# Four convolution shifts given to VectorE, the group norm ahead of the convolution's mean, quarter state updates and head sums in two parts

## The reference

```python
for l in range(2):
    x = x + 0.5 * swiglu(rms_norm(x), ...)           # 1024 -> 2816 -> 1024
    proj = rms_norm(x) @ w_in[l]                     # 2944 columns
    y_rwkv = rwkv7(token_shift(proj[:, :1280]))      # 6 heads of 64, recurrent state 64x64 a head
    y_attn = attention(proj[:, 1280:2432])           # 6 heads, q and k normed by head, 3 dilations
    y_conv = conv_mixer(proj[:, 2432:])              # 256 channels, causal depthwise, 31 taps
    x = x + concat(y_rwkv, y_attn, y_conv) @ w_out[l]
    x = x + 0.5 * swiglu(rms_norm(x), ...)

# rwkv step
state = state * w_t + (state @ a_t) b_t + v_t k_t ; y_t = state @ r_t
# then y is normed by head (mean and variance over 64), scaled, added to a bonus and gated
# conv_mixer
z = u[:, :256] * sigmoid(u[:, 256:])
z = sum_j w[j] * z shifted by (30 - j) tokens, plus a bias
z = silu(layer_norm(z))                              # over the 256 channels
```

## Time and profile before

| | |
|---|---|
| time, median of 3 runs | 1419.99 us (1418.55 to 1420.47) |
| profiled execution | 1419.94 us, of which the span is 1417.9 us |
| PE busy | 1375.2 us, 97% of the span |
| DVE busy | 937.0 us, 66% |
| ACT busy | 721.9 us, 51% |
| POOL busy | 172.5 us, 12%, 169 instructions |
| chain that ended last, by engine | PE 79%, POOL 10%, DVE 5%, ACT 3%, issue 2% |

### The profile page before, as it was taken

How to read it: one execution, slowest core, us unless ns; L and a number is a source line. 1 busy time by engine, 2 the same in 40 slices (tenths; PEclk the granted TensorE clock), 3 DMA queues, 4 the chain that set the end, 5 groups by cost and what they waited for, 6 DMA issues and landing times.

```text
span 1417.9 us, 25201 instructions
## 1 busy us (share of the span) xinstructions
PE 1375.2 (97%) x10047; PEld 1211.3 (85%) x10047; DVE 937.0 (66%) x1211; ACT 721.9 (51%) x992; POOL 172.5 (12%) x169
## 2 busy tenths in 40 slices
PE   8999999998999999999999999999999999999997
PEld 7888889977788888888888988788888898899996
DVE  5656666684766556665656766576565675887677
ACT  6444466454654445644447655464444445554442
POOL 3000000198000000000000059400000033000000
PEclk9999999999999999999999999999999999999999
DMA  9756365200676545755519210275562943455540
GB/s 339 249 180 201 98 202 163 82 18 2 218 253 199 185 144 180 247 191 179 176 65 297 75 61 3 87 258 193 186 198 100 315 154 116 149 186 199 179 147 30
DMA packets 172516, 230.58 MB, mean 163 GB/s; under 512 B 4671, under 2 KB 153847, under 8 KB 172181
## 3 DMA queue, kind: packets, MB, share of 16 engines
q1 hardware_dynamic: 169952, 223.75, 48.0%
q10 hardware_dynamic: 1877, 5.59, 1.0%
q0 software_dynamic: 608, 0.12, 0.0%
HBM read 228.39 MB, written 2.63 MB: 163 GB/s over the span
## 4 chain that ended last, share of the span: by engine, by line
PE 79%; POOL 10%; DVE 5%; ACT 3%; issue 2%; DMA 0%; POOLq 0%; DVEq 0%; ACTq 0%
PE bank L473 42%; PE bank L593 22%; PE bank L595 11%; POOL mix L1875 4%; POOL proj L1873 4%; ACT hT L870 1%; POOL mix L1869 1%; DVE up_lo L458 1%; ACT up_hi L453 1%; DVE down_lo L458 1%; PE bank L1161 1%; PE bank L1209 1%; DVE work L784 0%; DVE x L758 0%; PE bank L841 0%
## 5 line engine op out<-in xcount | busy, mean ns | idle before, releaser
L458 DVE TENSOR_TENSOR down_lo<-w_down,down_hi 128x2048 fp32r<-128x2048 f32 x67 | 155.3, 2318 | 100.5 <-ACT down_hi L453 100.5
L676 ACT ACTIVATE work<-bank 128x256 f32<-128x256 f32 x176 | 66.7, 384 | 266.8 <-PE bank L595 257.6
L453 ACT ACTIVATE down_hi<-w_down 128x2048 fp32r<-128x2048 f32 x67 | 128.6, 1919 | 121.4 <-PE bank L473 120.3
L458 DVE TENSOR_TENSOR gate_lo<-w_gate,gate_hi 128x2048 fp32r<-128x2048 f32 x67 | 153.9, 2297 | 53.1 <-ACT gate_hi L453 52.9
L593 PE MATMUL bank<-hT,up_hi 128*128 128x512 f32 x704 | 176.7, 393 | 0.8 <-DVE up_lo L458 0.8
L458 DVE TENSOR_TENSOR up_lo<-w_up,up_hi 128x2048 fp32r<-128x2048 f32 x72 | 162.4, 2256 | 17.0 <-ACT up_hi L453 17.0
L593 PE MATMUL bank<-hT,gate_hi 128*128 128x512 f32 x640 | 159.3, 391 | 0.0
L473 PE MATMUL bank<-down_hi,ff_hi 128*128 128x512 f32 x400 | 156.3, 391 | 0.0
L473 PE MATMUL bank<-down_lo,ff_hi 128*128 128x512 f32 x400 | 156.3, 391 | 0.0
L473 PE MATMUL bank<-down_hi,ff_lo 128*128 128x512 f32 x400 | 155.7, 389 | 0.0
L725 DVE TENSOR_TENSOR work<-bank,work 128x256 f32<-128x256 f32 x176 | 73.0, 420 | 114.5 <-ACT work L676 114.5
(11 more groups left out here) (340 smaller groups left out, 2389.0 us busy)
## 6 DMA issues: line engine op xcount, KB each, us to landing
w_gate<-in_ffn_w_gate_dram SPq DMA_DIRECT2D x44, 1024.0 KB, 5.4
w_up<-in_ffn_w_up_dram SPq DMA_DIRECT2D x44, 1024.0 KB, 5.4
w_down<-in_ffn_w_down_dram SPq DMA_DIRECT2D x44, 1024.0 KB, 5.1
w_up<-in_w_in_dram SPq DMA_DIRECT2D x12, 1024.0 KB, 9.5
w_down<-in_w_in_dram SPq DMA_DIRECT2D x11, 1024.0 KB, 6.4
w_gate<-in_w_up_dram SPq DMA_DIRECT2D x11, 1024.0 KB, 5.1
w_up<-in_w_up_dram SPq DMA_DIRECT2D x11, 1024.0 KB, 5.1
w_down<-in_w_down_dram SPq DMA_DIRECT2D x11, 1024.0 KB, 5.2
```

The lines of the kernel that those rows point to most:

```text
L453: act.activation(staged[kind][0][:, 0:cols], slot[sl][:, 0:cols], ACT.Copy).then_inc(high[sl], 1)
L458: dve.tensor_tensor(staged[kind][1][:, 0:cols], slot[sl][:, 0:cols], staged[kind][0][:, 0:cols].bitcast(F32), ALU.subtract).then_inc(split ...
L676: act.activation(low[:, q, j * SEQ:(j + 1) * SEQ], psum[2 * q + j][:, SEQ:], ACT.Copy)\
```

## The change

Line numbers in the changed file differ. The parts are:

1. Shifts 6 to 9 leave POOL. DVE computes them (`side_tap`) into `parts[1]`: the first as a product, the others as product and addition in one instruction, two channel blocks each. Two shifts follow the state update of chunk 0 and two that of chunk 1. POOL adds `parts[1]` to `acc` at its end.
2. In the output, PE does unit 1, `gn_spread(0)`, unit 2 and `gn_spread(1)` first, and the mean of the convolution after them. DVE subtracts that mean after the group norm's products. ACT squares both parities before it takes the first root. `cl_ready` is now `conv_dve`, with one more signal.
3. The state update goes by quarters. PE forms only the 64x64 block of each head (six products where there were three), DVE multiplies the two diagonal quarters with half the partitions each, `state` is cleared beforehand (a memset of 1152 columns), and `cend` shrinks from three arrays of 384 columns to one copy of 9.
4. The head sums of q stand in the middle of tile 8 and those of k in the middle of tile 9. `qk_sum` follows the latter.

```diff
--- before
+++ after
...
@@ -309,2 +309,3 @@
         SCALED_LAGS = (1, 2, 3, 4, 5)
+        SIDE_LAGS = (6, 7, 8, 9)
         parts = [proj[:, K + 1:K + 3, 1:], proj[:, V:V + 2, 1:]]
@@ -330,3 +331,3 @@
         satok, o = area(o, NT, 384)
-        cend, o = area(o_bh, 3, 3, P)
+        cend, o = area(o_bh, 3, 3)
         state, o = area(o, 3, 3, P)
@@ -1248,7 +1249,9 @@
             ones_product(pe, 4, bonus).then_inc(S["bonus_mm"], 1)
-            pe_tile(pe, uses, 8, n_norm)
+            def qk_sums(i):
+                return head_sums(pe, psum[3][:, 12 * i:12 * i + 12], lambda c, t: qsq[:, 3 * i + c, tokens(t)])
+
+            pe_tile(pe, uses, 8, n_norm, (0,))
             pe.wait_ge(S["qk_sq"], 1 + past["qk_sq"])
-            for i in range(2):
-                mm = head_sums(pe, psum[3][:, 12 * i:12 * i + 12], lambda c, t: qsq[:, 3 * i + c, tokens(t)])
-            mm.then_inc(S["qk_sum"], 1)
+            qk_sums(0)
+            pe_tile(pe, uses, 8, n_norm, (1,))
             pe.wait_ge(S["kk_ready"], 1 + past["kk_ready"])
@@ -1263,3 +1266,5 @@
                     mm.then_inc(S["a_mm"], 1)
-            pe_tile(pe, uses, 9, n_norm)
+            pe_tile(pe, uses, 9, n_norm, (0,))
+            qk_sums(1).then_inc(S["qk_sum"], 1)
+            pe_tile(pe, uses, 9, n_norm, (1,))
 
@@ -1400,11 +1405,9 @@
                                   stop=False, skip_group_check=True)
-                    for pr in range(3):
-                        at = slice(pr * P, (pr + 1) * P)
-                        pe.matmul(bank[:, at], tok[2][rows_, t, at], tok[3][rows_, t, at], start=(ch == 0 and pr == 0),
-                                  stop=False, skip_group_check=True)
+                    for h in range(NH1):
+                        pe.matmul(bank[half(h), head(h)], tok[2][rows_, t, head(h)], tok[3][rows_, t, head(h)],
+                                  start=(ch == 0 and h < 2), stop=False, skip_group_check=True)
                     pe.wait_ge(S["sa_done"], ch + 1 + past["sa_done"])
-                    for pr in range(3):
-                        at = slice(pr * P, (pr + 1) * P)
-                        mm = pe.matmul(bank[:, at], tok[1][rows_, t, at], satok[rows_, t, at], start=False, stop=True,
-                                       skip_group_check=True)
+                    for h in range(NH1):
+                        mm = pe.matmul(bank[half(h), head(h)], tok[1][rows_, t, head(h)],
+                                       satok[rows_, t, head(h)], start=False, stop=True, skip_group_check=True)
                     mm.then_inc(S["st_mm"], 1)
@@ -1457,3 +1460,6 @@
             variance(1)
+            out_unit(0, 1)
             gn_spread(0)
+            out_unit(0, 2)
+            gn_spread(1)
             pe.wait_ge(S["conv_acc"], 1 + past["conv_acc"])
@@ -1463,5 +1469,3 @@
             mm.then_inc(S["cl_mean"], 1)
-            out_unit(0, 1)
-            gn_spread(1)
-            for i in range(2, 7):
+            for i in range(3, 7):
                 out_unit(0, i)
@@ -1624,2 +1628,3 @@
                    .then_inc(S["y_sq"], 1)
+            for k in range(2):
                 act.wait_ge(S["gn_var"], k + 1 + past["gn_var"])
@@ -1637,3 +1642,3 @@
             act_high(act, uses, OUT_SLOTS[3], 0, 1)
-            act.wait_ge(S["cl_ready"], 2 + past["cl_ready"])
+            act.wait_ge(S["conv_dve"], 3 + past["conv_dve"])
             for c in range(2):
@@ -1794,9 +1799,19 @@
                     attention.normalise(h + 1)
-                if i in (19, 20, 21):
-                    c = i - 19
-                    if c == 0:
-                        dve.wait_ge(S["copy_done"], COPIES - 6 + past["copy_done"])
-                    end = ec[:, :, (c + 1) * CHUNK - 1:(c + 1) * CHUNK].broadcast_to([P, 3, P])
-                    dve.tensor_tensor(cend[:, c], end, pairs.unsqueeze(1).broadcast_to([P, 3, P]), mult)\
-                       .then_inc(S["cend_ready"], 1)
+                if i == 19:
+                    dve.wait_ge(S["copy_done"], COPIES - 6 + past["copy_done"])
+                    ends = ec.rearrange("p c (k n) -> p k c n", n=CHUNK)[:, 0:3, :, CHUNK - 1]
+                    dve.tensor_copy(cend, ends)
+                    dve.memset(state, 0.0).then_inc(S["cend_ready"], 1)
+
+            def side_tap(i):
+                lag = SIDE_LAGS[i]
+                for c in range(2):
+                    to, z, w = parts[1][:, c, lag:], proj[:, CU + c, 1:1 + SEQ - lag], col("conv_dw_w", 2 * (CONV_W - 1 - lag) + c)
+                    if i == 0:
+                        ins = dve.tensor_scalar(to, z, w, None, mult)
+                    else:
+                        ins = dve.scalar_tensor_tensor(to, z, w, to, mult, add)
+                if i + 1 < len(SIDE_LAGS):
+                    link(ins)
+                return ins
 
@@ -1807,5 +1822,16 @@
                 if ch == 0:
-                    dve.wait_ge(S["cend_ready"], 3 + past["cend_ready"])
-                dve.tensor_tensor(state[:, ch], src, cend[:, ch], mult).then_inc(S["st_done"], 1)
+                    dve.wait_ge(S["cend_ready"], 1 + past["cend_ready"])
+                for r in (half(0), half(1)):
+                    ins = dve.tensor_tensor(state[r, ch, :, r], src[r, :, r], cend[r, ch].unsqueeze(2).broadcast_to([CHUNK, 3, CHUNK]),
+                                            mult)
+                ins.then_inc(S["st_done"], 1)
                 dve.wait_ge(S["st_done"], ch + 1 + past["st_done"])
+                if ch == 0:
+                    dve.wait_ge(S["conv_added"], 2 + past["conv_added"])
+                    dve.memset(parts[1][:, :, 0:SIDE_LAGS[0]], 0.0)
+                    side_tap(0)
+                    side_tap(1)
+                if ch == 1:
+                    side_tap(2)
+                    side_tap(3).then_inc(S["conv_dve"], 1)
                 if ch == 2:
@@ -1823,6 +1849,2 @@
                                 over_heads(gnst[:, 6 * k:6 * k + 6], NH1)).then_inc(S["gn_rows"], 1)
-            dve.wait_ge(S["cl_mean"], 1 + past["cl_mean"])
-            for c in range(2):
-                ins = dve.scalar_tensor_tensor(mix[:, 6 + c, :], psum[0][:, 0:SEQ], -1.0 / 256, mix[:, 6 + c, :], mult, add)
-            ins.then_inc(S["cl_ready"], 1)
             for k in range(2):
@@ -1832,2 +1854,6 @@
                 dve.tensor_tensor(parity(mix[:, 0:3, :])[:, k], view, parity(bonus)[:, k], add).then_inc(S["mixr_ready"], 1)
+            dve.wait_ge(S["cl_mean"], 1 + past["cl_mean"])
+            for c in range(2):
+                ins = dve.scalar_tensor_tensor(mix[:, 6 + c, :], psum[0][:, 0:SEQ], -1.0 / 256, mix[:, 6 + c, :], mult, add)
+            ins.then_inc(S["conv_dve"], 1)
             for k in range(2):
@@ -1863,3 +1889,3 @@
             link(pool.tensor_tensor(acc, part, per_channel("conv_dw_b", 0, SEQ), add))
-            for lag in range(1, CONV_W):
+            for lag in (i for i in range(1, CONV_W) if i not in SIDE_LAGS):
                 n = SEQ - lag
@@ -1875,4 +1901,5 @@
                     link(pool.tensor_tensor(acc[:, :, lag:], acc[:, :, lag:], part[:, :, lag:], add))
-            pool.sem_inc(S["conv_acc"], 1)
-            pool.wait_ge(S["cl_ready"], 1 + past["cl_ready"])
+            pool.wait_ge(S["conv_dve"], 1 + past["conv_dve"])
+            pool.tensor_tensor(acc, acc, parts[1], add).then_inc(S["conv_acc"], 1)
+            pool.wait_ge(S["conv_dve"], 2 + past["conv_dve"])
             pool.tensor_tensor(proj[:, CG:CG + 2, 1:], acc, acc, mult).then_inc(S["cl_sq"], 1)
```

More of the change, by code:

```diff
@@ L167 @@
     "low_copied": 88, "summed": 88, "silu_done": 22, "ff_ready": 22, "x_updated": 12, "proj_ready": 0,
-    "dve_link": 33, "pool_link": 52, "scaled": 10, "shifted": 10, "copied": 7, "lora_acts": 2, "lora_mm": 1,
+    "dve_link": 36, "pool_link": 44, "scaled": 10, "shifted": 10, "copied": 7, "lora_acts": 2, "lora_mm": 1,
     "decay_sig": 3, "iclr_sig": 3, "gate_copied": 2, "cum_ready": 2, "exps_done": 3, "kk_sq": 1, "kk_sum": 1,
@@ L174 @@
     "pav_mm": 2, "pav_done": 2, "mat_mm": 2, "mat_done": 2, "sa_mm": 4, "sa_done": 4, "st_mm": 3, "st_done": 3,
-    "cend_ready": 3, "y_mm": 2, "y_sq": 2, "y_gated": 2, "gn_var": 2, "gn_root": 2, "gn_rows": 2, "gn_spread": 2,
+    "cend_ready": 1, "y_mm": 2, "y_sq": 2, "y_gated": 2, "gn_var": 2, "gn_root": 2, "gn_rows": 2, "gn_spread": 2,
     "mixr_ready": 2, "score_mm": 6, "biased": 6, "maxed": 6, "exp_done": 12, "p_ready": 6, "pt_mm": 6, "pt_done": 6,
@@ L178 @@
     "conv_part": 5, "conv_added": 5, "conv_acc": 1, "cl_mean": 1, "cl_sq": 1, "cl_var": 1, "cl_root": 1,
-    "cl_ready": 2, "mixc_ready": 2, "pool_ready": 0, "pool_mm": 0, "taps_act": 0, "taps_picked": 0, "lag_done": 0,
+    "conv_dve": 3, "mixc_ready": 2, "pool_ready": 0, "pool_mm": 0, "taps_act": 0, "taps_picked": 0, "lag_done": 0,
     "taps_done": 0, "stats_ready": 0, "lin_dve": 0, "lin_act": 0, "ln_first": 0,
@@ L225, in build @@
             gn_var gn_root gn_rows gn_spread mixr_ready score_mm biased maxed exp_done p_ready pt_mm pt_done av_mm
```

(2 more changed lines are left out.)

## The result

The changed kernel takes 1409.15 us (median) against 1420.23 us for the kernel before, measured beside it. The ratio is 0.9925, with a 95% interval of 0.9905 to 0.9944. Measured again later it was 1409.59 against 1420.18 us, ratio 0.9918 (0.9905 to 0.9931). The first median takes in one of four executions that took 1925.33 us at a mean clock of 0.651; the median of the other three is 1408.09 us. Forecast were 1407.3 us and 12.6 us less; by those three 12.1 us came, and 10.6 us in the later measurement. The profiled execution took 1410.21 us, of which the span is 1408.4 us (before 1419.94 and 1417.9).

What follows compares the result with a forecast made beforehand. PE, busy for 97% of the span, was taken to bound the kernel. Tail 7.4, head sums 2.7 and quarters 3.5 less 1.0 for shifts gave 12.6 us off 1419.94: 1407.3 us, range 1402.5 to 1414.5 us.

Steps and rivals of the forecast that it cites:

- The wait for POOL goes: Convolution wait in the tail: POOL ends near 339.5, some 5 us early, so PE's 3.07 us idle goes whole.
- The tail: one period at 1.2 GHz: First variance to slot 1 (T): 15.1 us becomes 11.4, with one slow-clock period; gain 3.7 us a layer.
- the first rival: In the tail PE stays at 2.4 GHz, without the slow period: 16.0 us gained, 1403.9 us; chance 0.23.
- Head sums: full clock, a new wait of 1.1 us: Around tile 9: full clock returns, PE newly waits for masks before the chunk products; net gain 0.6 and 2.1 us.
- Quarters: 1.75 us a layer: State updates in the recurrence: narrower products in five groups save 1.85 us, less 0.1 on DVE; 3.5 us in all.
- Shifts on DVE: Between state updates: shifts beside POOL make updates late, partly hidden by PE's products; loss 0.5 us a layer, 1.0 in all.
- The held rival: Recurrence: POOL holds each DVE shift 0.94 us, updates late by 5.1 us a layer; 1416.5 us, chance 0.08.
- No other place moves: Outside the tail, head sums and recurrence, including the untouched second block: forecast change 0.
- Slower, as the clock falls in the recurrence: Rival: PE at 1.2 GHz from first quarter update to output units, up to 15.2 us more a layer; chance 0.03.
- the sign that the prediction names: Test: prediction is wrong if the clock falls inside the recurrence, or the tail still takes over 13 us.

Runs made afterwards that it cites:

- tail reordered: Changed kernel with two DVE shifts, masks ahead of the inverse and values' products earlier, plus DVE's mean subtraction, POOL's square and PE's variance moved later: 1409.8 us, ratio 0.9933.
- old order: Changed kernel with PE's convolution mean back ahead of output units 1 and 2, and DVE's subtraction ahead of the group norm's products: 1410.37 us, ratio 0.9929.
- run with 10 taps: Changed kernel with POOL's shifts 10 to 30 left out, so POOL is idle while DVE does its four shifts: 1411.0 us.
- the repeat: Changed kernel measured and profiled again with no edit: 1409.59 us, ratio 0.9918.

## Why the prediction was right, and where it was off

- **The wait for POOL goes, with cover to spare.** Right. Forecast end of POOL 339.5, measured 339.54. Without the shifts, the same kernel waits 3.6 us a layer. The cover is 7 us and not the forecast 5 us, because the output starts 1.7 us later than forecast.
- **The tail: one period at 1.2 GHz.** The idle time went as forecast; the period at 1.2 GHz came in neither layer of this profile. T at full clock was forecast as 9.7 and is 10.3 us: the low parts (1.86 us for 1.23) were held beside POOL's square. With the tail reordered they last 1.23 us, and T less its new wait is 11.74 - 2.19 = 9.55 us. With the old order they last 1.23 us as well, but a product ahead of them is held in their place (1.04 us for 0.56) and T is 10.30 us. This profile followed the first rival. It isn't a rule: in twelve profiles PE waits at most 0.16 us for POOL's convolution (all but the kernel before and the one without shifts). Of their 24 tails 18 kept the full clock, and in the other six it fell although PE had no idle time in the tail ahead of it. Four of these six are among the ten tails of kernels in which the waits for the second and third update are gone or small, two among the fourteen others. That less waiting ahead of the tail brings the fall is possible and not shown.
- **Head sums: full clock, a new wait of 1.1 us.** Right: -0.52 and -2.03 us against -0.6 and -2.1, the wait 0.81 us. The clock held in all 22 layers with the sums apart.
- **Quarters: 1.75 us a layer.** Right: 1.83 us, once the shifts are away.
- **Shifts on DVE: "I take 0.5 us a layer".** This term failed. It is 2.22 us. The gaps were right (forecast 2.7 and 3.1 us, 2.79 and 2.81 us without shifts), and the holding nearly so: 0.5 us was taken for each instruction, 0.62 us came. Wrong was that PE's own products would hide two thirds of the lateness. From the first update to the second DVE took 1.66 us longer than without shifts, and from there to the third 1.20 us. PE had nothing in hand at the second and 0.8 us at the third, so 2.05 us in all reached it; the rest of the 2.22 us is the 0.17 us ahead of the recurrence.

  The reason given for the low price, that most of DVE's instructions of that kind are not held, was wrong too. In the kernel before, five instructions with both inputs in SBUF ran beside POOL that have a counterpart beside an idle one. Three were held: a mask with 1.36 us for 0.42, a product of 768 columns with 1.90 for 0.95, a low part with 3.20 for 2.29. Of the other two (0.49 for 0.42 and 0.96 for 0.96 us), the second held POOL in its turn: the addition beside it took 1.82 us, the one before it 1.08. The 768 columns before, and in the run with 10 taps:

```profile
293.69 1.90 DVE L1775 TENSOR_TENSOR work<-work,cst 128x768 f32<-128x768 f32 x1
...
292.67 0.95 DVE L1780 TENSOR_TENSOR work<-work,cst 128x768 f32<-128x768 f32 x1
```

  The held rival had the right mechanism, and with 5.1 us a layer too high a price. The Trainium skill's rule that DVE and GpSimd block each other for a whole instruction when DVE reads two SBUF inputs ("SBUF — State Buffer", "Who interferes with whom") agrees with the 0.98 us beside POOL and 0.44 us without it, for the fused form too. Why POOL's own instructions were hardly longer beside the shifts no run shows.
- **No other place moves.** Off by 1.6 us in this profile, for the period at 764.5. It stands behind narrow LoRA products that the change doesn't touch. The forecast priced the clock only where it fell before. Why it fell here in this execution and not in the repeat is open.
- **Slower, as the clock falls in the recurrence.** It fell there once (877 to 881), and the stretch was no longer for it, 68.90 in both layers: PE ran slower where it would have waited 1.61 us for DVE. The repeat shows the same at 332. By the sign that the prediction names, a fall of the clock inside the recurrence, it would be wrong; the sign was badly chosen, since such a fall cost nothing while DVE was late.

In sum: tails 9.56, head sums 2.55, quarters 3.66, less 4.44 for the shifts and 1.8 for the clock and the rest, is 9.5 us in the profile; forecast 7.4 + 2.7 + 3.5 - 1.0. That the total came as near as it did is partly luck: the tails gave 2.2 us more than forecast, and the recurrence 3.3 us less (a loss of 0.8 for a gain of 2.5).

## What to carry to other kernels

Work moved to DVE beside a busy POOL was two to three times its own duration here, with its inputs in SBUF (0.98 us for 0.44, 0.96 for 0.30). Price it so, and put it only where the gap holds that: two shifts fitted, four didn't. Ask of each gap what the next engine has in hand behind it: here it was nothing at the second update and 0.8 us at the third. Move only as much as removes the wait; the slack of 7 us that the four shifts made was paid for with 2.2 us a layer on the path. And when two edits share a stretch, measure each alone: the quarters' gain was real and was eaten by the shifts.

## What the runs showed of the hardware

The clock of PE fell with PE busy all the time (0.70 over 17 us with 48 narrow products in a row), and the same instructions kept it in one layer and lost it in the other. With the narrow products in two groups it held in 22 of 22 layers. Whole executions of one program differ by it: 1406.4 us at a mean clock of 0.997 and 1420.2 us at 0.985, the same kernel. Effects of under 2 us can be read here from a stretch of the trace at full clock, and not from the median; where DVE works beside POOL, even such a stretch differed by 1.0 us between the layers of one execution (69.27 and 70.30 us).

The holding between DVE and POOL was seen in both directions: DVE's shifts grew from 0.30 to 0.44 us to 0.96 to 1.16 us beside POOL, and POOL's square from 1.28 to 3.02 us beside a DVE subtraction of 2.28 us that had started 0.15 us earlier.
